# Two-layer transformer with a second mixer block on one core: in the MLP pairs, the high and low half of x go through one 512-column product, and two weight sums move from VectorE to GpSimd

## The chip, the cores and the metric

One core of one Trainium2 chip runs the whole program. The metric is the device time of one launch in microseconds (us); a lower time is better. Engines are called by the profile's names: PE is TensorE (matmul), PEld its weight loads, DVE is VectorE, ACT is ScalarE, POOL is GpSimd, SP the queue that issues most DMAs.

## The reference

The program takes 512 tokens of width 1024 through two layers (an attention mixer and a retention mixer, each followed by an MLP), a final norm, and a further block with a gated feed-forward before and after a sparse-attention and recurrent mixer. The change concerns the squared-ReLU MLP of the first two layers (width 1024, hidden 4096):

```python
def squared_relu_mlp(h, w_up, w_down):
    u = jax.nn.relu(h @ w_up)
    return (u * u) @ w_down
...
h = h + squared_relu_mlp(rms_norm(h, g_mlp[layer]), w_mlp_up[layer], w_mlp_down[layer])
```

All arithmetic is float32. The two gated feed-forward parts (`ffn1`, `ffn2`: silu(h @ w_gate) * (h @ w_up), then w_down, hidden 2816) share some of the code that is touched.

## The kernel before

**Numbers in two parts.** The fast matmul type (fp32r) keeps only part of a float32. So every operand is split: `hi` is the value rounded to fp32r by ScalarE, `lo` is value minus `hi` by VectorE, and a product is w_hi*x_hi + w_hi*x_lo + w_lo*x_hi.

**Pairs and units.** In `mlp0` and `mlp1` the first 8 of the 32 hidden blocks are computed densely. The other 24 blocks are taken in 12 pairs q per layer, by a Strassen-Winograd scheme with seven products, called units, in place of eight: unit p of pair q multiplies a form of the weights (a block, or a sum of blocks, 128 partitions x 512) with a form of x (four 128x256 parts: `x_hi`/`x_lo` for p = 1, 2, 4, the sums `xs_hi`/`xs_lo` for p = 5, 6, 3, 7). One unit in `up_unit` is 12 products of 256 columns: for each of four chunks form_hi * x_hi and form_hi * x_lo (L3134), then four times form_lo * x_hi (L3138). `ffn1` and `ffn2` have 18 such pairs each, made of a gate block and an up block.

**Order.** PE runs the units of a phase in the order of `up_phase`: (q,1), (q-1,4), (q-1,3), (q,2), (q,6), (q,5), (q,7), then (q+1,1), (q,4), (q,3) and so on. An MLP layer has three phases of four pairs. The last two units of a phase stand among the first products of the down projection (`down_part`, L3147, 512 columns); dense down products (L2835, L2840) follow. All waits are hand-written semaphore counts; each engine executes its own list in order.

**Weight forms.** SP loads the blocks of pair q into `forms[q % 2]` (L745 to L754; the last half that the accumulating DMA needs is L751, and it waits until the `lo` of unit (q-2,7) is made). POOL then issues a DMA that adds the second block onto them (`add_forms`, L2791). Two further forms are sums of forms: `third_form` (L1944, for unit 6) and `fourth_form` (L1949, for unit 4), one VectorE instruction of 512 columns each, written to the single buffer `form_sum`. `form_high` (L1039, ACT) writes `ring`, `form_low` (L1937, DVE) writes the `lo`, two units ahead of PE in `up_pairs`.

**Products out of PSUM.** Units 1, 6, 7, 4 of a pair accumulate one after the other in one bank; 2 has its own; 5 and 3 share one. ACT copies the bank after unit 1 (`first_copy`) and after unit 6 (`second_copy`, L1046). DVE makes `first_sum` (L1964, after unit 2), `fourth_sum` (after unit 7: a copy `third_copy` at L1972, then unit 5 minus it, L1974), and `third_sum` (L1980, after unit 3). ACT takes unit 4 straight out of PSUM through ReLU (L1063). Then come ReLU, square and `u_hi` on ACT, `u_lo` on DVE (`up_low`, L1987). PE's unit (q,4) may start only when the copy of (q,7) is made, since it adds onto the same bank; between (q,7) and (q,4) PE has one unit, (q+1,1).

Of the kernel before, what the change touches and what calls it, by code (L numbers as in the profile page):

```python
# [36 lines left out]
P = 128  # L37
# [92 lines left out]
def gates_before(q):  # L130

    return 3 * min(q, PAIR_FROM[2]) + 2 * max(q - PAIR_FROM[2], 0)

# [190 lines left out]
def build(nc, stream, params, tables, tables_ret, tables_mix, x_in, out):  # L324
    with ExitStack() as ctx:
# [15 lines left out]
        x_hi = sb("x_hi", [P, DC, T], F32R)  # L341
        x_lo = sb("x_lo", [P, DC, T], F32R)
# [23 lines left out]
        sq_lo = sb("sq_lo", [P, T], F32R, over=top - T * 4)  # L366
        inv = sb("inv", [P, T])
# [21 lines left out]
        xs_hi = sb("xs_hi", [P, 4, 4, HALF], F32R)  # L389
        xs_lo = sb("xs_lo", [P, 4, 4, HALF], F32R)  # L390
# [12 lines left out]
        third_copy = sb("third_copy", [P, HALF], over=std_final_at)  # L403
# [211 lines left out]
        def x_part(p, j, hi):  # L615
# [3 lines left out]
            return (xs_hi if hi else xs_lo)[:, j, (5, 6, 3, 7).index(p)]  # L619

# [200 lines left out]
        def _(act):  # L821
# [231 lines left out]
            def positive(layer, q, part):  # L1053

                to = up_sum[q % 2]
                made = layer * HIDDEN // P + chunk_of(layer, q, 0)
                if part == 0:
                    act.wait_ge(*upto("f_mm", UNIT_AT[q, 4] + 1))
                    if in_layer(q) >= 2:
                        act.wait_ge(sig("ul_done"), made - 4 + 1)  # L1060
                    else:
                        act.wait_ge(sig("ul_done"), made - 2 * in_layer(q))
                    nc.scalar.activation(to[0][:, HALF:T], ps[:, up_bank(q, 4), 0:HALF], ACT.Relu).then_inc(flag("f_pos"), 1)  # L1063
                elif part == 1:
                    act.wait_ge(*upto("f_ev", 4 * q + 1))
                    nc.scalar.activation(to[0][:, 0:HALF], to[0][:, 0:HALF], ACT.Relu).then_inc(flag("f_pos"), 1)
                else:
                    act.wait_ge(*upto("f_ev", 4 * q + 4))
# [85 lines left out]
            def gate_first(q):  # L1154

                act.wait_ge(*upto("f_ev", 4 * q + 1))
# [513 lines left out]
        def _(dve):  # L1670
# [269 lines left out]
            def third_form(q):  # L1940

                dve.wait_ge(sig(f"added_{q % 2}"), 16 * (q // 2 + 1))
                dve.wait_ge(*upto(f"a_in_{q % 2}", 16 * (q // 2 + 1)))
# [22 lines left out]
            def fourth_sum(layer, q):  # L1966

                if q:
                    dve.wait_ge(*upto("f_ev", 4 * q - 1))
# [1797 lines left out]
```

## Time and profile before

| | |
|---|---|
| median of 3 runs | 2407.51 us (2407.11 to 2408.11) |
| profiled execution | 2407.99 us, its span 2406.2 us |
| PE busy | 2393.8 us, 99% of the span |
| DVE busy | 1627.7 us, 68% |
| ACT busy | 1157.2 us, 48% |
| POOL busy | 155.1 us, 6% |
| granted TensorE clock | 1.00 throughout (the 2.4 GHz level) |
| up units in the MLP layers | 24 pairs x 7 units x 12 products |

A row of a timeline gives the start and the duration in us, the engine, the line, the operation with output <- input, shapes and a count where equal rows are merged, and in brackets the idle time before it with what ended it. The duration of a matmul is its latency: the next one starts long before it ends, so the cost of a product is the distance from start to start. The same holds for DVE instructions, to a smaller degree.

### The profile page before, as it was taken

The page shows a single profiled execution, that of the slowest core. Times are in us where ns is not written, and L with a number is a line of the kernel's source. Part 1 is how long each engine was busy: PE and PEld are TensorE (multiplying, and loading weights), DVE is VectorE, ACT ScalarE, POOL GpSimd, SP SyncE. Part 2 cuts the span into 40 slices and gives each one's busy share as a digit, 9 for nine tenths or more (in the row PEclk, how much of TensorE's full clock was granted, in tenths as well). Part 3 has the DMA queues.
Part 4 walks back from the last instruction along what each step waited for, and adds up shares of the span by engine and source line. Part 5 has one row for each costly group of instructions (what it writes and reads, how often), then busy time and mean ns, then how long its engine had stood idle before and what let it go on. Part 6 is the DMA issues. An engine that isn't in the chain of part 4 may idle for free.

```text
span 2406.2 us, 35737 instructions
## 1 busy us (share of the span) xinstructions
PE 2393.8 (99%) x13500; PEld 2063.6 (86%) x13500; DVE 1627.7 (68%) x2386; ACT 1157.2 (48%) x1837; POOL 155.1 (6%) x151
## 2 busy tenths in 40 slices
PE   9999999999999999999999999999999999999999
PEld 7777898998888888889998889998787778899998
DVE  6777765666656645756666977676968846867664
ACT  3565544554343443535645535454465453544443
POOL 2001000001000000100003000002000001000000
PEclk9999999999999999999999999999999999999999
DMA  4112443533222222444541555552222222455552
GB/s 141 66 66 70 149 149 108 155 106 105 97 79 81 77 79 96 142 133 137 149 132 62 153 153 167 141 158 86 79 71 71 71 70 97 149 158 166 141 154 83
DMA packets 108194, 273.50 MB, mean 114 GB/s; under 512 B 15120, under 2 KB 33808, under 8 KB 107920
## 3 DMA queue, kind: packets, MB, share of 16 engines
q1 hardware_dynamic: 95024, 237.97, 29.2%
q0 software_dynamic: 8640, 31.46, 7.7%
q10 hardware_dynamic: 4384, 2.10, 0.3%
q8 instruction: 94, 1.54, 0.3%
q14 instruction: 52, 0.43, 0.1%
HBM read 269.40 MB, written 2.10 MB: 113 GB/s over the span
## 4 chain that ended last, share of the span: by engine, by line
PE 92%; DVE 4%; issue 2%; ACT 1%; DMA 1%; POOL 1%; SPq 0%; ACTq 0%; DVEq 0%; POOLq 0%
PE ps L2835 29%; PE ps L3134 16%; PE ps L2840 14%; PE ps L3138 8%; PE ps L3147 6%; PE ps L3212 4%; PE ps L3513 2%; PE ps L2904 2%; PE ps L2888 2%; PE ps L3255 1%; PE ps L3039 1%; PE ps L3015 1%; PE ps L2992 1%; PE ps L3242 1%; DMA forms<-in_stream 1%
## 5 line engine op out<-in xcount | busy, mean ns | idle before, releaser
L836 ACT ACTIVATE w_hi<-raw 128x1024 fp32r<-128x1024 f32 x286 | 303.0, 1060 | 765.3 <-PE ps L2840 586.5
L1686 DVE TENSOR_TENSOR w_lo<-raw,w_hi 128x1024 fp32r<-128x1024 f32 x286 | 352.3, 1232 | 112.4 <-ACT w_hi L836 112.0
L2835 PE MATMUL ps<-x_hi,w_hi 128*128 128x512 f32 x848 | 337.2, 398 | 0.3 <-ACT w_hi L836 0.3
L2835 PE MATMUL ps<-x_lo,w_hi 128*128 128x512 f32 x848 | 330.6, 390 | 0.0
L2835 PE MATMUL ps<-u_hi,w_hi 128*128 128x512 f32 x642 | 250.5, 390 | 0.5 <-DVE h L1839 0.5
L2835 PE MATMUL ps<-u_lo,w_hi 128*128 128x512 f32 x642 | 249.9, 389 | 0.0
L3134 PE MATMUL ps<-xs_hi,ring 128*128 128x256 f32 x960 | 240.8, 283 | 1.1 <-ACT second_copy L1046 1.1
L3134 PE MATMUL ps<-xs_lo,ring 128*128 128x256 f32 x960 | 240.7, 283 | 0.0
L1039 ACT ACTIVATE ring<-forms 128x512 fp32r<-128x512 f32 x300 | 187.8, 629 | 92.5 <-PE ps L3138 90.7
L2840 PE MATMUL ps<-x_hi,w_lo 128*128 128x512 f32 x848 | 209.5, 389 | 0.0
L2835 PEld LDWEIGHTS ps<-x_hi,w_hi 128*128 128x128 f32 x848 | 159.3, 188 | 40.4 <-issue 5.8
L2835 PEld LDWEIGHTS ps<-x_lo,w_hi 128*128 128x128 f32 x848 | 159.3, 188 | 33.5 <-issue 1.7
L2840 PEld LDWEIGHTS ps<-x_hi,w_lo 128*128 128x128 f32 x848 | 159.2, 188 | 33.2
L3134 PEld LDWEIGHTS ps<-xs_hi,ring 128*128 128x128 f32 x960 | 184.3, 192 | 1.6 <-issue 1.5
L3134 PEld LDWEIGHTS ps<-xs_lo,ring 128*128 128x128 f32 x960 | 184.3, 192 | 0.1
L3134 PE MATMUL ps<-x_hi,ring 128*128 128x256 f32 x720 | 180.8, 283 | 0.9 <-DVE x_lo L2178 0.6
L3134 PE MATMUL ps<-x_lo,ring 128*128 128x256 f32 x720 | 180.6, 283 | 0.0
L2840 PE MATMUL ps<-u_hi,w_lo 128*128 128x512 f32 x642 | 159.0, 389 | 0.0
L1937 DVE TENSOR_TENSOR ring_b<-forms,ring 128x512 fp32r<-128x512 f32 x224 | 152.5, 684 | 4.2 <-ACT ring L1039 3.9
L2835 PEld LDWEIGHTS ps<-u_hi,w_hi 128*128 128x128 f32 x642 | 120.5, 188 | 26.2 <-DVE h L1839 0.9
L2840 PEld LDWEIGHTS ps<-u_hi,w_lo 128*128 128x128 f32 x642 | 120.5, 188 | 25.0
L2835 PEld LDWEIGHTS ps<-u_lo,w_hi 128*128 128x128 f32 x642 | 120.5, 188 | 24.9
(476 smaller groups left out, 4598.6 us busy)
## 6 DMA issues: line engine op xcount, KB each, us to landing
raw<-in_stream SPq DMA_DIRECT2D x293, 512.0 KB, 3.6
forms<-in_stream SPq DMA_DIRECT2D x180, 256.0 KB, 4.3
forms<-in_stream SPq DMA_DIRECT2D x60, 512.0 KB, 4.7
forms<-in_stream POOLq DMA_DIRECT2D x60, 512.0 KB, 5.7
x_tok<-in_x SPq DMA_DIRECT2D x4, 512.0 KB, 7.2
out_x<-xn ACTq DMA_DIRECT2D x7, 256.0 KB, 2.3
tab_ret<-in_tables_ret SPq DMA_DIRECT2D x1, 1536.0 KB, 6.3
raw<-in_stream SPq DMA_DIRECT2D x3, 256.0 KB, 3.2
```

The lines of the kernel that those rows point to most:

```text
L836: nc.scalar.activation(w_hi[:, slot(n)], raw[:, slot(n)], ACT.Copy).then_inc(hi_done, 1)
L1039: nc.scalar.activation(form_hi[form_slot(v)], form_of(q, p), ACT.Copy).then_inc(flag("f_hi"), 1)
L1686: nc.vector.tensor_tensor(w_lo[:, slot(n)], raw[:, slot(n)], w_hi[:, slot(n)].bitcast(F32), ALU.subtract).then_inc(lo_done, 1)
L1937: nc.vector.tensor_tensor(form_lo[form_slot(v)], form_of(q, p), form_hi[form_slot(v)].bitcast(F32), ALU.subtract).then_inc(flag("f_lo"), 1)
L2835: nc.tensor.matmul(ps[:, gemm_bank(n)], w_hi[:, s, k], x(k), start=(k == 0 and i == 0), stop=False)
L2840: last = nc.tensor.matmul(ps[:, gemm_bank(n)], w_lo[:, s, k], hi(k), start=False, stop=(k == kc - 1))
L2888: return nc.tensor.transpose(dst, src, ident)
L2904: return nc.tensor.matmul(ps[:, VALUE_BANKS[g][tb]], x[:, c, tb * P:(tb + 1) * P], w[:, slot(n), PAIRS * k:PAIRS * (k + 1)].rearrange("p i ...
L3134: nc.tensor.matmul(bank, form_hi[s][:, j * P:(j + 1) * P], x_part(p, j, i == 0), start=(p in (1, 2, 5) and j == 0 and i == 0), stop=False, ...
L3138: last = nc.tensor.matmul(bank, form_lo[s][:, j * P:(j + 1) * P], x_part(p, j, True), start=False, stop=(j == 3), skip_group_check=True)
L3147: last = nc.tensor.matmul(ps[:, gemm_bank(n)], w[:, slot(n), k], x[:, 0, k], start=(k == 0 and i == 0), stop=(k == kc - 1 and i == 2))
L3212: return nc.tensor.matmul(ps[:, RET_BANKS[tb]], x[:, c, tb * P:(tb + 1) * P], weights, start=(c == 0 and w is w_hi and x is x_hi), stop=(c ...
```

## The change

In the MLP layers, five of the seven units (1, 2, 6, 7, 4) become two-sided: x_hi and x_lo, now halves of one tensor, are the moving operand of one 512-column product with form_hi, so that w_hi*x_hi lands in the left half of the PSUM bank and w_hi*x_lo in the right half. The products form_lo * x_hi stay at 256 columns and add onto the left half. The two halves are then added: `first_sum` and `third_sum` become two dependent VectorE instructions each, `fourth_sum`'s copy becomes a `tensor_reduce` over the two halves, and a new `second_sum` does the same for unit 4, whose ReLU on ACT then reads SBUF. ACT's two copies are 512 wide. `third_form` and `fourth_form` move from VectorE's list to GpSimd's, behind the DMA issue of the same pair and ahead of that of the next, in all four layers with pairs. Semaphore counts are adapted. The core of the diff:

```diff
+def sums_before(q):
+    return 7 * min(q, PAIR_FROM[2]) + 4 * max(q - PAIR_FROM[2], 0)
...
-        x_hi = sb("x_hi", [P, DC, T], F32R)
-        x_lo = sb("x_lo", [P, DC, T], F32R)
+        x_two = sb("x_two", [P, 2, DC, T], F32R)
+        x_hi, x_lo = x_two[:, 0], x_two[:, 1]
...
-        xs_hi = sb("xs_hi", [P, 4, 4, HALF], F32R)
-        xs_lo = sb("xs_lo", [P, 4, 4, HALF], F32R)
+        xs_two = sb("xs_two", [P, 2, 4, 4, HALF], F32R)
+        xs_hi, xs_lo = xs_two[:, 0], xs_two[:, 1]
...
-        third_copy = sb("third_copy", [P, HALF], over=std_final_at)
+        first_wide = sb("first_wide", [P, T], over=sq_new_at)
+        second_wide = sb("second_wide", [P, T], over=std_final_at)
+        third_fold = sb("third_fold", [P, HALF], over=inv_at)
...
+        def x_both_parts(p, j):
+            if p in (1, 2, 4):
+                return x_two[:, :, j + (0 if p == 1 else KC // 2), (HALF if p == 4 else 0):(T if p == 4 else HALF)]
+            return xs_two[:, :, j, (5, 6, 3, 7).index(p)]
...
             def copy_of(q, p):
+                if layer_of(q) < 2:
+                    if q:
+                        act.wait_ge(*upto("f_ev", sums_before(q - 1) + (1 if p == 1 else 7)))
+                    nc.scalar.activation((first_wide if p == 1 else second_wide)[:], ps[:, up_bank(q, p)],
+                                         ACT.Copy).then_inc(flag("f_copy"), 1)
...
             def positive(layer, q, part):
                 if part == 0:
-                    act.wait_ge(*upto("f_mm", UNIT_AT[q, 4] + 1))
-                    nc.scalar.activation(to[0][:, HALF:T], ps[:, up_bank(q, 4), 0:HALF], ACT.Relu).then_inc(flag("f_pos"), 1)
+                    act.wait_ge(*upto("f_ev", sums_before(q) + 5))
+                    nc.scalar.activation(to[0][:, HALF:T], to[0][:, HALF:T], ACT.Relu).then_inc(flag("f_pos"), 1)
...
+            def folded(to, wide):
+                nc.vector.tensor_reduce(to, wide.rearrange("p (a f) -> p f a", a=2), AX_X, ALU.add).then_inc(flag("f_ev"), 1)
+            def second_sum(q):
+                whole = wide_of(q, 4)
+                dve.wait_ge(*upto("f_ev", sums_before(q) + 2))
+                folded(up_sum[q % 2][0][:, HALF:T], whole)
...
             def first_sum(layer, q):
-                nc.vector.tensor_tensor(up_sum[q % 2][0][:, 0:HALF], product_of(q, 2), first_copy[:], ALU.add).then_inc(flag("f_ev"), 1)
+                to = up_sum[q % 2][0]
+                nc.vector.tensor_tensor(to, wide_of(q, 2), first_wide[:], ALU.add).then_inc(flag("f_ev"), 1)
+                dve.wait_ge(*upto("f_ev", sums_before(q) + 1))
+                nc.vector.tensor_tensor(to[:, 0:HALF], to[:, 0:HALF], to[:, HALF:T], ALU.add).then_inc(flag("f_ev"), 1)
...
             def fourth_sum(layer, q):
-                nc.vector.tensor_copy(third_copy[:], product_of(q, 7)).then_inc(flag("f_ev"), 1)
-                dve.wait_ge(*upto("f_ev", 4 * q + 2))
-                nc.vector.tensor_tensor(up_sum[q % 2][1][:, HALF:T], product_of(q, 5), third_copy[:], ALU.subtract).then_inc(
+                folded(third_fold[:], wide_of(q, 7))
+                dve.wait_ge(*upto("f_ev", sums_before(q) + 3))
+                nc.vector.tensor_tensor(up_sum[q % 2][1][:, HALF:T], product_of(q, 5), third_fold[:], ALU.subtract).then_inc(
...
             def third_sum(q):
-                nc.vector.tensor_tensor(up_sum[q % 2][1][:, 0:HALF], product_of(q, 3), second_copy[:], ALU.subtract).then_inc(
+                nc.vector.tensor_tensor(to, product_of(q, 3), second_wide[:, 0:HALF], ALU.subtract).then_inc(flag("f_ev"), 1)
+                dve.wait_ge(*upto("f_ev", sums_before(q) + 6))
+                nc.vector.tensor_tensor(to, to, second_wide[:, HALF:T], ALU.subtract).then_inc(flag("f_ev"), 1)
...
                     if before[1] == 2:
                         first_sum(layer, before[0])
+                    if before[1] == 4:
+                        second_sum(before[0])
...
-                    if p == 4 and q + 1 < (layer + 1) * UP_PAIRS:
-                        third_form(q + 1)
...
-                    if p == 3 and q + 1 < (layer + 1) * UP_PAIRS:
-                        fourth_form(q + 1)
...
+            def third_form(q):
+                pool.wait_ge(sig(f"added_{q % 2}"), 16 * (q // 2 + 1))
+                pool.wait_ge(*upto(f"a_in_{q % 2}", 16 * (q // 2 + 1)))
+                if in_layer(q):
+                    pool.wait_ge(*upto("f_lo", UNIT_AT[q - 1, 6] + 1))
+                    pool.wait_ge(*upto("f_sum", 2 * q))
+                nc.gpsimd.tensor_tensor(form_sum[:, 0], forms[q % 2][:, 3], forms[q % 2][:, 0], ALU.add).then_inc(flag("f_sum"), 1)
+            def fourth_form(q):
+                pool.wait_ge(*upto("f_sum", 2 * q + 1))
+                if in_layer(q):
+                    pool.wait_ge(*upto("f_lo", UNIT_AT[q - 1, 4] + 1))
+                nc.gpsimd.tensor_tensor(form_sum[:, 1], forms[q % 2][:, 1], form_sum[:, 0], ALU.add).then_inc(flag("f_sum"), 1)
...
                 for q in range(PAIR_FROM[layer], PAIR_FROM[layer + 1]):
                     add_forms(q)
+                    third_form(q)
+                    fourth_form(q)
...
+                two_sided = wide and p in (1, 2, 6, 7, 4)
...
                 if p == 4:
-                    pe.wait_ge(*upto("f_ev", 4 * q + 2))
+                    pe.wait_ge(*upto("f_ev", sums_before(q) + (3 if wide else 2)))
...
                 for j in range(4):
+                    if two_sided:
+                        nc.tensor.matmul(both, form_hi[s][:, j * P:(j + 1) * P], x_both_parts(p, j),
+                                         start=(p in (1, 2) and j == 0), stop=False, skip_group_check=True)
-                    for i in range(2):
+                    for i in range(0 if two_sided else 2):
                         nc.tensor.matmul(bank, form_hi[s][:, j * P:(j + 1) * P], x_part(p, j, i == 0),
                                          start=(p in (1, 2, 5) and j == 0 and i == 0), stop=False, skip_group_check=True)
```

## Rows read from the trace of the kernel before

**Rows 1.** The page's part 1: busy us, share of the span, instructions.
```profile
PE 2393.8 (99%) x13500; PEld 2063.6 (86%) x13500; DVE 1627.7 (68%) x2386; ACT 1157.2 (48%) x1837; POOL 155.1 (6%) x151
```

**Rows 2.** Waits of PE by line, whole run: us, times, longest; largest in pairs.
```profile
PE ps L3134 <- ACT second_copy L1046: 1.1, 2, 0.6
```

**Rows 3.** Windows, first MLP phase: us, busy us of each engine, clock, DMA.
```profile
332.50:372.70 40.20, 40.20 (x325) 39.71 (x325) 32.16 (x57) 29.94 (x58) 3.45 (x4) 1.00 0.67 187
```

**Rows 4.** Timeline of PE: starts of units, of dense blocks, and between both.
```profile
359.91 0.28 PE L3134 MATMUL ps<-x_hi,ring 128*128 128x256 f32 x1
...
361.35 0.28 PE L3134 MATMUL ps<-x_hi,ring 128*128 128x256 f32 x1
...
369.99 1.09 PE L3147 MATMUL ps<-u_hi,w_hi 128*128 128x512 f32 x4
...
374.17 0.28 PE L3134 MATMUL ps<-xs_hi,ring 128*128 128x256 f32 x1
...
383.80 0.39 PE L2835 MATMUL ps<-u_hi,w_hi 128*128 128x512 f32 x1
...
389.24 0.39 PE L2835 MATMUL ps<-u_hi,w_hi 128*128 128x512 f32 x1
...
606.90 1.98 PE L3212 MATMUL ps<-w_hi,x_hi 128*128 128x512 f32 x8
608.72 1.98 PE L3212 MATMUL ps<-w_hi,x_lo 128*128 128x512 f32 x8
```

**Rows 5.** Timeline of DVE, around the end of unit (2,7) at 359.91.
```profile
358.16 0.69 DVE L1937 TENSOR_TENSOR ring<-form_sum,ring 128x512 fp32r<-128x512 f32 x1 [0.65 <-ACT ring L1039]
358.77 0.69 DVE L1987 TENSOR_TENSOR u_lo<-inv_final,u_hi 128x512 fp32r<-128x512 f32 x1
360.21 0.43 DVE L1972 COPY third_copy<-ps 128x256 f32<-128x256 f32 x1 [0.75 <-PE ps L3138]
360.67 0.43 DVE L1974 TENSOR_TENSOR inv_final<-ps,third_copy 128x256 f32<-128x256 f32 x1
361.01 0.68 DVE L1937 TENSOR_TENSOR ring_b<-forms,ring 128x512 fp32r<-128x512 f32 x1
361.61 0.68 DVE L1944 TENSOR_TENSOR form_sum<-forms 128x512 f32<-128x512 f32 x1
```

**Rows 6.** Timelines of POOL and DVE where additions of both meet.
```profile
236.65 0.74 DVE L1713 SCALAR_TENSOR_TENSOR x_lo<-h,prm,x_hi 128x512 fp32r<-128x512 f32 x1
...
236.69 1.85 POOL L2786 TENSOR_TENSOR rstd<-rstd,xn 128x512 f32<-128x512 f32 x1 [3.57 <-ACT xn L857]
...
237.31 1.51 DVE L1869 TENSOR_TENSOR x_sum<-x_fp 128x256 f32<-128x256 f32 x1
...
1293.46 1.29 POOL L2786 TENSOR_TENSOR sq_new<-sq_new,xn 128x512 f32<-128x512 f32 x1
...
1293.68 0.69 DVE L1885 TENSOR_TENSOR down<-ps,inv_sq 128x512 f32<-128x512 f32 x1 [1.33 <-PE ps L2840]
...
1294.47 0.83 DVE L1887 TENSOR_TENSOR h<-h,down 128x512 f32<-128x512 f32 x1
```

**Rows 7.** Load of pair 3 (SP), its adding DMA (POOL), and L2791's landing times.
```profile
346.86 0.33 SPq L751 DMA_DIRECT2D forms<-in_stream  x1
...
352.21 0.86 POOL L2791 DMA_DIRECT2D forms<-in_stream  x1 [8.04 <-DMA forms<-in_stream]
...
DMA to landing us min/median/max: 5.1/5.7/8.8
```

**Rows 8.** Same, pair 4: load issue on SP and adding DMA on POOL.
```profile
356.94 0.33 SPq L751 DMA_DIRECT2D forms<-in_stream  x1
...
360.88 0.86 POOL L2791 DMA_DIRECT2D forms<-in_stream  x1 [7.80 <-DMA forms<-in_stream]
```

**Rows 9.** Timeline at the phase's end: last u_lo, and the product that needs it.
```profile
378.33 0.69 DVE L1987 TENSOR_TENSOR u_lo<-u,u_hi 128x512 fp32r<-128x512 f32 x1 [1.43 <-ACT u_hi L1082]
...
380.39 0.39 PE L3147 MATMUL ps<-u_hi,w_hi 128*128 128x512 f32 x1
```

**Rows 10.** Timeline of DVE in ffn1: the copy after unit 7 there.
```profile
1501.42 0.42 DVE L2077 COPY last_copy<-ps 128x256 f32<-128x256 f32 x1 [0.75 <-PE ps L3138]
```

More of the change, by code:

```diff
@@ L366, in build @@
         sq_lo = sb("sq_lo", [P, T], F32R, over=top - T * 4)
+        inv_at = where[0]
         inv = sb("inv", [P, T])
@@ L1154, in gate_first @@
             def gate_first(q):
-                act.wait_ge(*upto("f_ev", 4 * q + 1))
+                act.wait_ge(*upto("f_ev", sums_before(q) + 1))
                 part = gate_up[q % 2][0][:, 0:HALF]
@@ L1938, in form_low @@
                                         ALU.subtract).then_inc(flag("f_lo"), 1)
-            def third_form(q):
-                dve.wait_ge(sig(f"added_{q % 2}"), 16 * (q // 2 + 1))
-                dve.wait_ge(*upto(f"a_in_{q % 2}", 16 * (q // 2 + 1)))
-                nc.vector.tensor_tensor(form_sum[:, 0], forms[q % 2][:, 3], forms[q % 2][:, 0], ALU.add).then_inc(flag("f_sum"), 1)
-            def fourth_form(q):
-                dve.wait_ge(*upto("f_sum", 2 * q + 1))
-                nc.vector.tensor_tensor(form_sum[:, 1], forms[q % 2][:, 1], form_sum[:, 0], ALU.add).then_inc(flag("f_sum"), 1)
             def product_of(q, p):
@@ L2021, in up_pairs @@
                 if more:
-                    third_form(q + 1)
                     form_low(v + 3)
+                second_sum(q)
                 third_sum(q)
@@ L2026, in up_pairs @@
                 up_low(layer, q, 1)
-                if more:
-                    fourth_form(q + 1)
             def mlp(first, chunks_before, norm, next_norm):
@@ L2047, in mlp @@
                         x_forms(norm, c + 2)
-                third_form(layer * UP_PAIRS)
-                fourth_form(layer * UP_PAIRS)
                 form_low(UNIT_FROM[layer])
@@ L2115, in gate_pairs @@
                         up_first_sum(before[0])
-                    if p == 4 and q + 1 < PAIR_FROM[layer + 1]:
-                        third_form(q + 1)
                     if v + 2 < end and v + 2 > UNIT_FROM[layer] + 3:
                         form_low(v + 2)
-                    if p == 3 and q + 1 < PAIR_FROM[layer + 1]:
-                        fourth_form(q + 1)
                     if p == 6 and q > qs[0]:
@@ L2138, in gate_pairs @@
                     form_low(v + 2)
-                    third_form(q + 1)
                     form_low(v + 3)
@@ L2143, in gate_pairs @@
                 hidden_low(layer, q)
-                if more:
-                    fourth_form(q + 1)
             def x_normed(layer, norm, j, parts):
@@ L2214, in ffn @@
                         x_gate_forms_low(layer, 3)
-                        third_form(PAIR_FROM[layer])
                         for i in range(3):
@@ L2220, in ffn @@
                         form_low(v + 3)
-                        fourth_form(PAIR_FROM[layer])
                     dve.wait_ge(sig("ul_done"), CHUNKS_FROM[layer] + c)
@@ L3107, in up_unit @@
                 q, p = UNITS[v]
-                bank = ps[:, up_bank(q, p), 0:HALF]
+                bank, both = ps[:, up_bank(q, p), 0:HALF], ps[:, up_bank(q, p)].rearrange("p (a f) -> p a f", a=2)
                 layer = layer_of(q)
+                wide = layer < 2
+                two_sided = wide and p in (1, 2, 6, 7, 4)
                 two_back = q - 2 if in_layer(q) >= 2 else None
```

40 lines of the change are left out of this document (19 added, 21 removed).

## The prediction

> **What bounds the kernel now.** I read the engine shares first [rows 1]: PE is busy 99% of the span, DVE 68%. Durations of matmuls overlap, so "busy" alone doesn't prove that PE never waits; the list of PE's waits does. Its largest entry in the pair units is 1.1 us in two places [rows 2]. In the first MLP phase (units of pairs 0 to 3) PE is busy 40.20 of 40.20 us and DVE 32.16, which is 80% [rows 3]. So these phases are bound by how fast PE starts products, and DVE is the next engine, with 20% to spare.
>
> The price of a product is the distance between starts, not the 0.28 or 0.39 us that a row prints. A unit starts at 359.91 and the next at 361.35: 1.44 us for 12 products of 256 columns, 120.0 ns each. A dense block starts at 383.80 and the next at 389.24: 5.44 us for 24 products of 512 columns, 226.7 ns each [rows 4]. The difference, 106.7 ns, is 256 columns at 2.4 GHz, the level at which the clock stands [rows 3]. What is left is 13.3 ns per product, whatever its width. Someone who takes 2 x 0.28 - 0.39 = 0.17 us from the durations would expect 480 x 0.17 = 82 us from this change; those durations contain the pipeline's latency, which is paid once per stream.
>
> **1. Merged products.** Removed: in 24 pairs, 5 units each, 8 products of 256 become 4 of 512. 4 x (2 x 120.0 - 226.7) = 53 ns per unit, and 120 units make 6.4 us. That is the upper end. Against it stands the change of width inside a unit. Between 369.99 and 374.17 PE runs 12 products of 512 and 12 of 256, entered from 256: 4.18 us, where 12 x 226.7 + 12 x 120.0 = 4.16 [rows 4]. So a change to 512 and back costs about 20 ns, and each merged unit has one. 53 - 20 = 33 ns, x 120 = 4.0 us, the value I take, because it is the only row with such a change. The moving operand now comes in two pieces of 256. The nearest row is L3212, whose moving operand is cut into four pieces: 8 products in 1.82 us, 227.5 ns each [rows 4], so pieces cost nothing visible. New lengths: a merged unit 1.407 us, a pair 5 x 1.407 + 2 x 1.44 = 9.92 us in place of 10.08.
>
> The Trainium skill, in "TensorE: Matmul & The Clock Gate", section "Back-to-back issue gap", gives 131 ns as the sustained spacing at 512 columns and 81 ns at 128; a straight line between them puts 256 near 98 ns, and merging would save 65 ns x 480 = 31 us, called an estimate from that page. The same section's other formula, N/2.4 + 2.5 ns, would make it 2.5 ns x 480 = 1.2 us. The trace agrees with neither: it shows 226.7 and 120.0, and the sum goes by those.
>
> **2. DVE's list in an MLP pair.** Start-to-start prices [rows 5]: an addition of 512 columns 0.60 us (361.01 to 361.61), of 256 columns 0.34 (360.67 to 361.01), and 0.12 more where the next one needs its result (360.21 to 360.67 is 0.46). A 512-column step that reads PSUM has the same duration, 0.69, as one that doesn't [rows 6], so I give it 0.60 too. Before: 7 `form_low`, 2 `up_low`, 2 form sums, 11 x 0.60 = 6.60; the copy 0.46; three sums 1.02; together 8.08 of 10.08, which is the 80% of rows 3. After: 9 x 0.60 = 5.40; `first_sum` 0.60 + 0.12 + 0.34 = 1.06; `fourth_sum` 0.72 + 0.34 = 1.06; `second_sum` 0.60; `third_sum` 0.46 + 0.34 = 0.80. Together 8.92 of 9.92. That fits, with 1.0 us left.
>
> No row shows a `tensor_reduce`. Its floor is what the copy of half the width costs (0.34), since it reads twice as much; its ceiling I set at double the 512-column addition, 1.20. I take 0.60, the row for the same number of elements read. The Trainium skill, in "VectorE: DVE Perf Modes", section on the perf-mode tier table, lists `tensor_reduce` as running at the plain rate only; no run here shows it.
>
> **3. The two form sums on POOL.** Alone, a POOL addition of 512 columns takes 1.28 to 1.29 us (1293.46). What matters is what it does to DVE. POOL starts one at 236.69 while DVE runs L1713, and takes 1.85: it waited about 0.57. The next DVE addition, at 237.31, takes 1.51 us where a 256-column one takes 0.43 [rows 5, 6]: it stood still about 1.09 us. L1887 at 1294.47 takes 0.83 in place of 0.69 and gets going 1.15 us after POOL's start. But L1885 at 1293.68, which reads PSUM and one SBUF operand, takes its normal 0.69 in the midst of POOL's addition [rows 6]. So: a POOL addition shuts out DVE steps with two SBUF inputs for about 1.14 us; the one that starts first goes first; steps out of PSUM pass. The Trainium skill states this rule in "SBUF — State Buffer", section "Who interferes with whom", and adds that `tensor_reduce` never contends on this chip; the first part agrees with rows 6, the second no run here shows.
>
> DVE thus gives up 2 x 0.60 and may get back 2 x 1.14 = 2.28 us of standing still per pair. If all of it falls on steps with two SBUF inputs, DVE needs 8.92 + 2.28 = 11.20 us in a pair of 9.92, and DVE is the bound. If it falls on DVE's idle time and on its steps out of PSUM (together about 1.0 + 2.8 us of a pair), it is free.
>
> **When POOL runs them.** `third_form` of pair q starts when the added block has landed: L751 to the POOL issue is 5.35 us for pair 3 and 3.94 for pair 4, and the landing takes 5.7 more [rows 7, 8]. L751 goes out when the `lo` of (q-2,7) is ready, so the landing is about 0 to 2 us before unit (q,1) starts. That is where DVE has its idle time (0.65 before 358.16, 0.75 before 360.21 [rows 5]) but also two `lo` steps, and behind them the step with the tightest due time. This step is the sum over (q,7)'s halves. PE has one unit, now 1.407 us, to run before (q,4). DVE wakes 0.30 us after the end of (q,7) (359.91 to 360.21 [rows 4, 5]), and the reduce takes 0.69 and some 0.05 for the signal: 1.04. It may start at most 0.37 us late before PE waits.
>
> I walked DVE's, POOL's and PE's lists through a phase with these prices. Pairs 0 and 1: no wait; `fourth_form(1)` meets the PSUM steps. Pair 2, with its landing early or late, puts DVE behind, and `fourth_form(3)`, which waits for the `lo` of (2,4), can only start just as DVE reaches (2,7)'s sum. The `up_low` ahead of that sum is held, and PE waits 0.04, 0.22 or 1.31 us at (2,4), by whether pair 3's block lands before or after DVE passes (3,1). At (3,4) four chunks of the down projection, 12 x 0.227 = 2.7 us, cover the delay. I take 0.7 us per phase, the middle; 6 phases make +4.2 us.
>
> **4. Other edits.** ACT: two copies 256 wider, about +0.25 us each, in a list that is busy 29.94 of 40.20 [rows 3]; covered. Unit 4's ReLU now stands behind DVE's `second_sum`, and behind it on ACT are `form_high` of (q,5) and (q,7); in my walk they are ready 0.4 us ahead of need. If DVE falls back more than that, PE waits here too. POOL's next DMA issue stands behind `fourth_form`; it moves by at most 1 us, which only shifts the landing. End of a phase: `third_sum` is 0.46 longer and the last u_lo ends at 379.02, needed at 380.39 [rows 9]: 1.37 in hand, 0. `ffn1`/`ffn2`: 36 pairs lose 1.2 us of DVE work and gain the 2.28; the copy after unit 7 waits 0.75 us on PE there and takes only 0.42 [rows 10], and PE's unit is still 1.44, so 0.
>
> **Sum.** 2407.99 - 4.0 + 4.2 = 2408.2 for the profiled execution, which stands 0.5 above the median: 2407.7 us.
>
> **Rivals.**
> A, the forecast: gain and waits cancel, 2403 to 2412. Chance 0.47.
> B, POOL's additions find the gaps: no late sum. For it: both idle stretches of DVE lie where the block lands [rows 5]. Then -4.0 to -6.4: 2401.1 to 2403.5. Chance 0.23; the part beyond -4.8 us is 0.13.
> C, DVE becomes the bound (slower). Place: the sum over (q,7)'s halves, behind held `lo` steps. It decides once more than 1.0 us of the 2.28 falls on steps with two SBUF inputs. The stretches between the first three sums of a phase are uncovered: 2 x (11.20 - 9.92) - 0.37 = 2.2 us per phase, 13 in all, less 4.0: 2416.7. Against it: 2.8 us per pair are PSUM steps that pass. Chance 0.18.
> D, the reduce costs 1.20: then 0.30 + 1.29 + 0.05 = 1.64 us stand against 1.407 even when DVE is idle, and DVE's list grows by 1.2: 18 uncovered sums at about 1 us each, less 4.0: about 2421. Chance 0.08.
> E, the 512-column product with two halves is no cheaper than two: gain 0, waits 4.2: 2411.7. Against it L3212. Chance 0.04, counted as no change.
>
> **Range and chances.** A measurement of this kernel can tell about 0.2%, 4.8 us, from no change. Faster by more: 0.13, from B. Slower: C and D, 0.26. Within: 0.61. 2402 leaves out the best part of B (under 0.1), 2419 leaves out D and the far end of C (about 0.1).
>
> **What would show it.** Right: merged products 227 ns apart, unit starts 1.39 to 1.41 apart, PE's waits on the sum over (q,7) 1 us or less at the third pair of a phase. DVE rows with two SBUF inputs of up to 1.8 us beside POOL's additions. Wrong: unit starts 1.44 apart (E); PE waits at every pair (C); a reduce of over 0.8 us (D); no waits (B). A wait of PE on `form_high` would be a miss of part 4.

## The result, and the profile of the changed kernel

The changed kernel takes 2420.18 us (median of 4 runs, 2417.2 to 2422.2); beside it the kernel before took 2407.69 (2407.1 to 2408.1). The ratio is 1.0052, with a 95% interval of 1.004 to 1.0063: slower by 0.5%, and 1.2 us above the upper end of the range that I gave (2402 to 2419). The profiled execution has a span of 2420.0 us, against 2406.2 before: 13.8 us more. The changed kernel also spreads over 5 us from run to run, where the one before spreads over 1. Of the eleven executions of four_early_dve below, two took 3381 and 8462 us; they are left out of its median.

The page's part 1, which answers to [rows 1]: PE has 480 products fewer, DVE is busy 39 us longer although 120 form sums have left it for 72 new steps, and POOL has doubled.

```profile
PE 2394.9 (99%) x13020; PEld 2039.2 (84%) x13020; DVE 1666.6 (69%) x2338; ACT 1160.6 (48%) x1837; POOL 329.3 (14%) x271
```

The list of PE's waits, which answers to [rows 2] (us in total, times, longest). All of these waits are new. L3162 is the merged product, L3178 the down projection's `down_part`, L3165 an unmerged product, L2861 a dense block.

```profile
PE ps L3162 <- ACT second_wide L1061: 4.1, 5, 1.2
PE ps L3178 <- DVE u_lo L2010: 4.0, 4, 1.8
...
PE ps L3162 <- DVE third_fold L1966: 1.9, 4, 0.6
PE ps L2861 <- DVE u_act L1712: 1.3, 1, 1.3
...
PE ps L3165 <- DVE last_copy L2094: 1.1, 2, 0.6
```

The window of [rows 3], the first MLP phase. PE had been busy for all of its 40.20 us, DVE for 32.16 and POOL for 3.45.

```profile
332.50:372.70 40.20, 38.45 (x242) 34.19 (x241) 37.95 (x59) 29.90 (x56) 12.93 (x11) 1.00 0.68 182
```

PE around unit (2,7), which answers to [rows 4]. A row of L3162 holds a unit's four merged products, one of L3169 its low group. The unit begun at 360.54 is followed by the next at 361.94, 1.40 us later: merging works as priced. But (2,7), at 359.08, waited 1.17 us.

```profile
357.27 0.64 PE L3169 MATMUL ps<-xs_two,ring_b 128*128 128x256 f32 x4
359.08 1.16 PE L3162 MATMUL ps<-xs_two,ring 128*128 128x512 f32 x4 [1.17 <-ACT second_wide L1061]
360.07 0.64 PE L3169 MATMUL ps<-xs_two,ring_b 128*128 128x256 f32 x4
360.54 1.09 PE L3162 MATMUL ps<-x_two,ring 128*128 128x512 f32 x4
361.47 0.63 PE L3169 MATMUL ps<-x_two,ring_b 128*128 128x256 f32 x4
361.94 1.09 PE L3162 MATMUL ps<-x_two,ring 128*128 128x512 f32 x4
```

What made it wait, read backwards over three engines. ACT made `second_wide` at 358.36, the eighth of a chain of steps without a gap that began at 355.12. There ACT had stood 1.71 us, since its list has unit 4's relu next, and that one needs DVE's `second_sum`:

```profile
352.26 0.64 ACT L1053 ACTIVATE ring<-form_sum 128x512 fp32r<-128x512 f32 x1 [0.92 <-POOL form_sum L2809]
...
355.12 0.42 ACT L1077 ACTIVATE u<-u 128x256 f32<-128x256 f32 x1 [1.71 <-DVE u L1966]
355.44 0.62 ACT L1053 ACTIVATE ring<-forms 128x512 fp32r<-128x512 f32 x1
...
358.36 0.57 ACT L1061 ACTIVATE second_wide<-ps 128x512 f32<-128x512 f32 x1
```

DVE (first three rows) took from 350.40 to 354.41 for two `form_low` (printed as one row of x2) and one `up_low`: 4.0 us for 3 x 0.60. POOL (last two) ran both form sums in that time.

```profile
350.40 2.38 DVE L1951 TENSOR_TENSOR ring_b<-forms,ring 128x512 fp32r<-128x512 f32 x2
352.70 1.78 DVE L2010 TENSOR_TENSOR u_lo<-u_act,u_hi 128x512 fp32r<-128x512 f32 x1
354.41 0.68 DVE L1966 TENSOR_REDUCE u<-ps 128x256 f32<-128x512 f32 x1
...
350.80 1.42 POOL L2809 TENSOR_TENSOR form_sum<-forms 128x512 f32<-128x512 f32 x1 [6.91 <-DMA forms<-in_stream]
352.30 1.63 POOL L2816 TENSOR_TENSOR form_sum<-forms,form_sum 128x512 f32<-128x512 f32 x1
```

The excess is 2.2 us for two additions, 1.1 each: the price of [rows 6]. Nothing of these two additions fell into a gap. ACT also waited 0.92 us, until 352.26, for the first form sum itself, but after that it still stood 1.71 us for DVE's `second_sum`: the late form sum is not what set the time here.

The second place is the end of a phase. In phase 2 of the second layer PE wants its first `down_part` at 1195.77, after the low group of (19,7) begun at 1195.29. It gets `u_lo` at 1197.7, since POOL's `fourth_form` (1195.45) holds the `up_low` that makes it. The DVE step two places ahead (1193.51) had already taken 1.79 us beside POOL's `third_form`, which began at 1193.47; so both additions of the pair stand in this wait:

```profile
1193.51 1.79 DVE L1951 TENSOR_TENSOR ring_b<-form_sum,ring 128x512 fp32r<-128x512 f32 x1
...
1195.83 1.75 DVE L2010 TENSOR_TENSOR u_lo<-u,u_hi 128x512 fp32r<-128x512 f32 x1
...
1195.45 1.58 POOL L2816 TENSOR_TENSOR form_sum<-forms,form_sum 128x512 f32<-128x512 f32 x1 [0.69 <-DVE ring_b L1951]
...
1197.73 1.15 PE L3178 MATMUL ps<-u_hi,w_hi 128*128 128x512 f32 x4 [1.80 <-DVE u_lo L2010]
1198.72 1.68 PE L3178 MATMUL ps<-u_lo,w_hi 128*128 128x512 f32 x4
1200.19 1.91 PE L3178 MATMUL ps<-u_hi,w_lo 128*128 128x512 f32 x4
1201.90 1.32 PE L3162 MATMUL ps<-x_two,ring 128*128 128x512 f32 x4
```

After this wait the products themselves are slow, and the window shows why: the last but two column, the mean granted clock, is 0.58 there: for most of the stretch it stood at 1.2 GHz and not at 2.4.

```profile
1199.00:1203.00 4.00, 4.00 (x12) 3.15 (x11) 2.17 (x4) 0.00 (x0) 0.00 (x0) 0.58 0.77 131
```

### The profile page after: what moved, and what is told of

Same layout as the page of the kernel before. It is cut to its first block, busy times and chain, and to the rows that moved or that the text cites. A ratio compares the mean times of both kernels' runs of the same rounds, so it can differ in the third digit from the quotient of the medians.

```text
span 2420.0 us, 34960 instructions
## 1 busy us (share of the span) xinstructions
PE 2394.9 (99%) x13020; PEld 2039.2 (84%) x13020; DVE 1666.6 (69%) x2338; ACT 1160.6 (48%) x1837; POOL 329.3 (14%) x271
## 4 chain that ended last, share of the span: by engine, by line
PE 89%; DVE 6%; issue 2%; ACT 2%; POOL 1%; DMA 0%; ACTq 0%; DVEq 0%; SPq 0%; POOLq 0%
PE ps L2861 29%; PE ps L2866 14%; PE ps L3165 11%; PE ps L3169 7%; PE ps L3178 6%; PE ps L3243 4%; PE ps L3162 3%; PE ps L3544 2%; PE ps L2930 2%; PE ps L2914 2%; PE ps L3286 1%; PE ps L3065 1%; DVE ring_b L1951 1%; PE ps L3041 1%; PE ps L3018 1%
## 5 line engine op out<-in xcount | busy, mean ns | idle before, releaser
L2861 PE MATMUL ps<-x_two,w_hi 128*128 128x512 f32 x1696 | 410.0, 394 | 2.1 <-DVE u_act L1712 1.3
L2861 PEld LDWEIGHTS ps<-x_two,w_hi 128*128 128x128 f32 x1696 | 315.0, 188 | 76.0 <-issue 9.1
L2861 PE MATMUL ps<-u_hi,w_hi 128*128 128x512 f32 x642 | 250.5, 390 | 0.3 <-DVE h L1853 0.3
L2861 PE MATMUL ps<-u_lo,w_hi 128*128 128x512 f32 x642 | 249.9, 389 | 0.0
L3165 PE MATMUL ps<-xs_two,ring 128*128 128x256 f32 x1536 | 215.6, 283 | 1.1 <-ACT second_copy L1065 1.1
L2866 PE MATMUL ps<-x_two,w_lo 128*128 128x512 f32 x848 | 209.5, 389 | 0.0
L3165 PEld LDWEIGHTS ps<-xs_two,ring 128*128 128x128 f32 x1536 | 198.0, 192 | 1.6 <-issue 1.5
L2809 POOL TENSOR_TENSOR form_sum<-forms 128x512 f32<-128x512 f32 x60 | 87.8, 1463 | 803.7 <-DVE ring_b L1951 514.1
L2866 PEld LDWEIGHTS ps<-x_two,w_lo 128*128 128x128 f32 x848 | 159.2, 188 | 33.1
L2861 PEld LDWEIGHTS ps<-u_hi,w_hi 128*128 128x128 f32 x642 | 120.5, 188 | 25.9 <-DVE h L1853 0.7
L2861 PEld LDWEIGHTS ps<-u_lo,w_hi 128*128 128x128 f32 x642 | 120.5, 188 | 24.9
L3165 PE MATMUL ps<-x_two,ring 128*128 128x256 f32 x864 | 121.7, 284 | 2.0 <-DVE last_copy L2094 1.1
L3169 PE MATMUL ps<-xs_two,ring_b 128*128 128x256 f32 x760 | 121.9, 283 | 0.0
L3165 PEld LDWEIGHTS ps<-x_two,ring 128*128 128x128 f32 x864 | 112.0, 192 | 3.9 <-issue 3.1
```

The costliest lines, as they stand in the source:

```text
L2809: nc.gpsimd.tensor_tensor(form_sum[:, 0], forms[q % 2][:, 3], forms[q % 2][:, 0], ALU.add).then_inc(flag("f_sum"), 1)
L2861: nc.tensor.matmul(ps[:, gemm_bank(n)], w_hi[:, s, k], x(k), start=(k == 0 and i == 0), stop=False)
L2866: last = nc.tensor.matmul(ps[:, gemm_bank(n)], w_lo[:, s, k], hi(k), start=False, stop=(k == kc - 1))
L3165: nc.tensor.matmul(bank, form_hi[s][:, j * P:(j + 1) * P], x_part(p, j, i == 0), start=(p in (1, 2, 5) and j == 0 and i == 0), stop=False, ...
L3169: last = nc.tensor.matmul(bank, form_lo[s][:, j * P:(j + 1) * P], x_part(p, j, True), start=False, stop=(j == 3), skip_group_check=True)
```

## The experiments

Below, H is the theory that POOL's additions hold DVE's steps with two SBUF inputs, and L that DVE's own new list is too long. Line numbers of a fence are those of that kernel. Beside these runs the kernel before stood at 2407.1 to 2407.5 us.

**pool_write_only.** Is it the addition on POOL, or only that POOL does something?

```diff
-nc.gpsimd.tensor_tensor(form_sum[:, 0], forms[q % 2][:, 3], forms[q % 2][:, 0], ALU.add).then_inc(flag("f_sum"), 1)
+nc.gpsimd.memset(form_sum[:, 0], 0.5).then_inc(flag("f_sum"), 1)
```

(the same for `form_sum[:, 1]`)

> The changed kernel with GpSimd's two additions per pair replaced by fills of the same 512 columns, which read nothing from SBUF. Waits and order stay as they are; the two form sums are left out (units 6 and 4 use a constant). Theory H: steps of VectorE keep their 0.6 us beside them, no waits of PE in the pairs, 2403 to 2405 us. Theory L: 2412 or more, as VectorE's list is unchanged.

Measured: 2402.25 us (2401.7 to 2403.0), ratio 0.9978 [0.9969, 0.9988], span 2401.2. As H said. None of PE's waits above is left. The page's part 1, then DVE in the stretch shown above, with both writes of POOL in it:

```profile
PE 2389.1 (99%) x13020; PEld 2037.3 (85%) x13020; DVE 1605.3 (67%) x2338; ACT 1163.1 (48%) x1837; POOL 217.4 (9%) x271
```

```profile
350.38 1.28 DVE L1951 TENSOR_TENSOR ring_b<-forms,ring 128x512 fp32r<-128x512 f32 x2
351.58 0.68 DVE L2010 TENSOR_TENSOR u_lo<-u_act,u_hi 128x512 fp32r<-128x512 f32 x1
352.18 0.68 DVE L1966 TENSOR_REDUCE u<-ps 128x256 f32<-128x512 f32 x1
...
350.83 0.53 POOL L2809 MEMSET form_sum<- 128x512 f32 x1 [6.69 <-DMA forms<-in_stream]
351.41 0.53 POOL L2816 MEMSET form_sum<- 128x512 f32 x1
```

The same three steps take 1.80 us instead of 4.01, and no single `form_low` or `up_low` of this trace prints more than 0.69 us. DVE is busy 1605.3 us in all, 61.3 less than with additions, or 0.51 us for each of the 120: almost half of the 1.14 that one can cost. This run also splits the change in two. Set against the kernel before, the difference of unit starts goes from -0.35 us at the first unit, (0,1), to -4.98 at (24,5), the first unit behind the MLP layers: 4.6 us for 120 merged units, 0.039 each. Set against the changed kernel the span is 18.8 us shorter; 0.6 us of that lies in a stretch of `ffn1` that varies between traces anyway (see the table below), the rest where the additions stand. A write is shorter than an addition too (0.53 against 1.28 us), so this run alone can't tell a held DVE from a form sum that is merely made earlier. The rows above can: the steps that PE waited for are DVE's own, 1.1 us too long each. A GpSimd instruction of 1.28 us that reads no SBUF was not run.

**pool_copy_only.** Does a POOL instruction with one input hold DVE too?

```diff
-nc.gpsimd.tensor_tensor(form_sum[:, 0], forms[q % 2][:, 3], forms[q % 2][:, 0], ALU.add).then_inc(flag("f_sum"), 1)
+nc.gpsimd.tensor_copy(form_sum[:, 0], forms[q % 2][:, 3]).then_inc(flag("f_sum"), 1)
```

(and `forms[q % 2][:, 1]` into `form_sum[:, 1]`)

> The changed kernel with GpSimd's two additions a pair replaced by copies of one input of 512 columns (the sums are left out, the forms themselves are passed on). With plain writes in their place the time was 2402.25 us and VectorE was not held. Theory R (a GpSimd instruction that reads SBUF holds VectorE's two-input steps, however many inputs it has): VectorE's steps show 1.3 us and more again and the time is above 2408 us. Theory R2 (only GpSimd's two-input instructions do): 2402 to 2403 us.

Measured: 2404.57 us (2403.6 to 2405.9), span 2402.5. Neither theory's number: a copy does hold DVE, as R says, but it takes only 0.61 us and so costs little, 2.3 us more than plain writes. The page, and the same place once more, DVE then POOL:

```profile
PE 2389.1 (99%) x13020; PEld 2037.3 (85%) x13020; DVE 1621.0 (67%) x2338; ACT 1162.0 (48%) x1837; POOL 248.2 (10%) x271
```

```profile
350.29 1.64 DVE L1951 TENSOR_TENSOR ring_b<-forms,ring 128x512 fp32r<-128x512 f32 x2
...
350.17 0.61 POOL L2816 COPY form_sum<-forms 128x512 f32<-128x512 f32 x1
```

DVE's pair takes 1.64 us instead of 1.28, and its busy time rises by 15.7 us, 0.13 for each copy. R2, "only two-input instructions hold", is refuted; R was right on the hold and wrong on the time.

**merged_dve_forms.** The merged products without POOL: both form sums back in DVE's list at their old places.

```diff
+                    if p == 4 and q + 1 < (layer + 1) * UP_PAIRS:
+                        third_form(q + 1)
                     if v + 2 < end:
                         form_low(v + 2)
+                    if p == 3 and q + 1 < (layer + 1) * UP_PAIRS:
+                        fourth_form(q + 1)
...
```

(and likewise at a phase's end and in `ffn1` and `ffn2`; GpSimd's two calls are gone)

> The changed kernel with the two form sums back on VectorE, as in the kernel before; the 512-column products and the longer sums stay. Theory H (GpSimd's additions hold VectorE's steps with two SBUF inputs): nothing is held any more, so PE's waits in the MLP phases go and the 4 us of the merged products remain: 2403 to 2406 us. Theory L (VectorE's own list has become too long): its list is 8.92 + 2 x 0.60 = 10.12 us against a pair of 9.92, longer than in the changed kernel without holding, so it stays at 2412 or more.

Measured: 2409.8 us (2409.0 to 2411.8), ratio 1.0011 [1.0001, 1.002], span 2407.4: between both theories. There is one new kind of wait, six times, once at the first `down_part` of each phase; its list row, then DVE and PE at the first of them:

```profile
PE ps L3205 <- DVE u_lo L2021: 3.5, 6, 0.6
```

```profile
369.10 0.68 DVE L2021 TENSOR_TENSOR u_lo<-u,u_hi 128x512 fp32r<-128x512 f32 x1
...
369.93 1.16 PE L3205 MATMUL ps<-u_hi,w_hi 128*128 128x512 f32 x4 [0.59 <-DVE u_lo L2021]
```

DVE's list is 8.92 + 1.20 = 10.12 us against a pair of 9.92. The lag grows by 0.2 us a pair, and the phase's first down chunks meet it. So L has a share too, which the changed kernel hides, as POOL has taken the 1.20 us away. DVE is busy 1673.6 us in this run: the 120 form sums are worth 68.3 us of it (1605.3 with writes on POOL), and on POOL their hold put 61.3 back, so the move relieved DVE by 7 us in all.

**pool_forms_only.** The other half alone: the kernel before, with `third_form` and `fourth_form` called from POOL's `add_layer`.

> The kernel before with only the two form sums moved to GpSimd; products and sums as before. Theory H: VectorE needs 6.88 + 2.28 = 9.16 us of 10.08, so most pairs don't wait, but u_lo and the lo of forms next to a phase's end and the dense blocks at the start of ffn2 are still held: 2410 to 2414 us. Theory L: VectorE's list is shorter than ever, nothing waits: 2407.5 or a little less.

Measured: 2410.98 us (2410.4 to 2412.9), ratio 1.0015 [1.0006, 1.0025], span 2408.6. As H said, and at one of the two places that it named, the start of `ffn2`; at the phases' ends the list shows no wait. In the MLP pairs DVE's list of 8.08 less 1.20, 6.88 us, leaves room for the 2.28. The loss is in the gated layers: `last_copy` (1.1 us in two waits) and the dense start of `ffn2` (1.3 and 0.8).

**pool_mlp_only.** The changed kernel with the form sums of `ffn1` and `ffn2` on DVE again.

```diff
-                    third_form(q)
-                    fourth_form(q)
+                    if layer < 2:
+                        third_form(q)
+                        fourth_form(q)
...
```

(the rest puts the calls back into VectorE's lists of `ffn1` and `ffn2`)

> The changed kernel with the form sums on GpSimd only in the two MLP layers and on VectorE in ffn1 and ffn2. In the trace of the changed kernel PE is 10.5 us behind the kernel before when ffn1's pairs begin and 13.8 us at the end. Theory H: the 3.3 us of ffn1 and ffn2 go, 2416 to 2418 us. Theory L (all of it in the MLP layers' sums, the rest chance): no change from 2420.

Measured: 2418.57 us (2414.6 to 2419.2), ratio 1.0046 [1.0029, 1.0063], span 2412.8. The gated layers' waits are gone. The medians of this kernel and the change differ by 1.6 us only and their runs overlap, so this time doesn't decide between the two theories, and the waits' price is read from the traces.

**early_low_dve.** merged_dve_forms with one step earlier:

```diff
-                    if p == 7 and q > qs[0] + 1:
+                    if p == 5 and q > qs[0] + 1:
                         up_low(layer, q - 2, 1)
```

> The merged products with the form sums on VectorE (2409.8 us), and the step up_low(q - 2, 1) moved in VectorE's list from the turn of unit (q, 7) to that of (q, 5). Nothing is left out. Theory P (place): the six waits of 0.53 to 0.60 us at the first chunks of the down projection stand there only because this step comes after form_low and fourth_sum in the list, though its input was ready four units earlier; they go, and the time is 2409.8 - 3.5 = 2406.3 us, faster than before by about 1 us. Theory L (load): VectorE's list of 10.12 us a pair is longer than the pair of 9.92 us, so the lateness comes up at another step instead: 2408.5 to 2410 us, and new waits on folded or form_lo in the last pair of each phase.

Measured: 2405.45 us (2404.8 to 2407.0), ratio 0.9994 [0.9984, 1.0003], span 2403.5. The six waits are gone, for 4.4 us, and P holds. The lag is not: each phase gains 0.3 to 0.4 us on the kernel before, where the run with plain writes gains 0.75 to 0.80, and it loses 0.10 to 0.27 us at a time at its last unit 7 and unit 4.

**early_low_pool, act_later_pool, both_moves_pool.** The same move in the changed kernel; ScalarE's side moved instead, as below; and both.

```diff
-                    if before and before[1] == 4:
-                        positive(layer, before[0], 0)
+                    if q > qs[0] and p == 5:
+                        positive(layer, q - 1, 0)
+                        squared(q - 1, 0)
                     if v + 3 < end:
                         form_high(v + 3)
...
-                    if q > qs[0] and p == 6:
-                        squared(q - 1, 0)
```

> The changed kernel, form sums on GpSimd, with up_low(q - 2, 1) moved from the turn of unit (q, 7) to that of (q, 5) in VectorE's list. Nothing is left out. Theory P: the waits of the first down chunks on u_lo (4.0 us in all) and the low clock behind the longest of them (about 1.6 us) go, and the time is 2420.2 - 5.6 = 2414.6 us. Theory S (shared debt): VectorE, held by GpSimd's additions, is late whichever step is asked for first; the wait that goes there comes back at the fold or at the copy of unit 6 some microseconds later, and the time stays at 2417 us or more.

> The changed kernel with ScalarE's positive(q - 1, 0) moved in its list from the turn of unit (q - 1, 3) to that of (q, 5), behind the copy of unit (q, 6), and squared(q - 1, 0) right behind it. Nothing is left out. Theory P: unit (q, 7) no longer waits for VectorE's second_sum through ScalarE's list; the four or five waits of 1.2 us (4.1 us in all) go, and the time is 2420.2 - 4.1 = 2416.1 us. Theory S: VectorE's lateness is then met by the fold at (q, 4) or by u_lo, which is made later too as its high half is later, and the time stays at 2418 us or more.

> The changed kernel with both moves: up_low(q - 2, 1) earlier in VectorE's list and positive(q - 1, 0) later in ScalarE's. Nothing is left out. Theory P: places add up, 2420.2 - 4.1 - 5.6 = 2410.5 us, with fold waits of about 2 us and those of the two gated layers left. Theory S: less than the sum of the two single moves, 2415 us or more.

Measured: 2415.6 us (2413.4 to 2416.2), 2420.65 (2418.3 to 2422.5) and 2414.73 (2412.6 to 2416.8). Their waits of PE in the lists, in this order:

```profile
PE ps L3162 <- ACT second_wide L1061: 5.7, 8, 1.2
...
PE ps L3178 <- DVE u_lo L2010: 0.5, 1, 0.5
```

```profile
PE ps L3177 <- DVE u_lo L2009: 6.0, 6, 1.8
PE ps L3161 <- DVE third_fold L1965: 4.8, 6, 1.6
```

```profile
PE ps L3161 <- DVE third_fold L1965: 2.9, 6, 1.5
...
PE ps L3177 <- DVE u_lo L2009: 1.9, 5, 0.6
```

The earlier `up_low` gives 4.6 us, nearer to the 5.6 of theory P than to S, although the waits on `second_wide` grow from 4.1 to 5.7. Taking away ACT's way gives nothing: its 4.1 us come back at the fold and at `u_lo`, as theory S said. Both together give 5.5 us, not 9.7. So the way through ACT was where PE first met DVE's lateness, and not a cost beside it. What is left, 7 us and more above the kernel before, is the lateness itself.

**four_merged_dve, four_merged_pool.** Less work for DVE: unit 4 keeps its eight products of 256 columns, ACT's relu reads it from PSUM as before, `second_sum` is gone, and the counts of DVE's sums go from 7 to 6 a pair. The line that chooses the units:

```diff
...
-                two_sided = wide and p in (1, 2, 6, 7, 4)
+                two_sided = wide and p in (1, 2, 6, 7)
...
```

> Form sums on VectorE, up_low where the change has it, but only four of the seven units merged (1, 2, 6, 7): unit 4 keeps its two products of 256 columns and ScalarE's relu takes it from PSUM as before, so VectorE's second_sum of 0.60 us a pair is not there. Nothing is left out. Theory L (VectorE's own list sets the end of a phase): its list is 9.52 us against a pair of about 9.96, no lag builds up, and the time is that of before less 24 x 4 x 0.035 = 3.4 us, 2404 us, with no loss at units (3, 7) and (3, 4). Theory P (only the place of up_low): the place is the old one here, so the waits of 0.5 to 0.6 us at the first down chunks are there again, and the time is 2406.5 to 2408 us.

> The same four merged units with the form sums on GpSimd as the change has them. Nothing is left out. Theory L: what VectorE lacks is time, 8.32 us of its own and 2 x 1.14 us held, 10.6 us a pair against 11.2 with five units; half of the lag of 1.24 us a pair is gone and the time falls to 2411 to 2415 us. Theory S (the hold falls where it hurts, whatever the sum): the fold and u_lo wait as before and only the way through ScalarE is gone, 2417 to 2419 us.

Measured: with the sums on DVE 2405.05 us (2404.3 to 2405.9), ratio 0.9989 [0.998, 0.9998]; with them on POOL 2414.94 (2409.6 to 2417.0), ratio 1.003 [1.0019, 1.004]. Both are nearer to L. The first is 4.8 us better than five merged units with the same places, though it merges less; no wait is listed in the MLP phases, and the units gain 0.15 us a pair. But L's "no loss" is not quite so: at the last unit 4 of each phase 0.15 to 0.19 us is lost, as the first down chunks still come 0.1 us late. The second is 5.2 us better than the change, at the upper end of the range that L gave; waits of 2.7 us on `u_lo` and 1.5 on the fold remain.

**four_early_dve.** Both remedies: four merged units, the form sums on DVE, `up_low` at `p == 5`.

> Four merged units (1, 2, 6, 7), form sums on VectorE, and up_low(q - 2, 1) moved from the turn of unit (q, 7) to that of (q, 5). Nothing is left out. With four units merged alone, the first down chunks of a phase still started 0.10 us late (369.48 after a group of 256 columns begun at 368.90, where 0.48 is the step), right at the end of that u_lo. Theory P (the place is a cost of its own, beside the load): the six starts gain 0.1 us each and what follows them another 0.07, and the time is 2404 to 2404.7 us. Theory L (with the list short enough the place is worth nothing): no change from 2405.05 us.

Measured: 2403.27 us (2403.05 to 2404.08), ratio 0.9984 [0.9974, 0.9994], span 2402.3. P holds, and the time is below even its range: 1.8 us below four_merged_dve, of which its starts and what follows them give 0.17 us a phase, 1.0 in all; the rest was not traced. This is the best version that computes everything: 0.16% faster than before, and 0.7% faster than the change. Set against the kernel before, unit starts move from +0.26 us at the first unit to -3.27 at (24,5), 3.5 us for 96 merged units, and each phase gains 0.59, so none of it is lost at a phase's end.

## Why the prediction was wrong, point by point

The span grew by 13.8 us; the sum had +0.2. Where the additions' 18.8 us fall, read as the difference of unit starts between the changed kernel and the one that only writes:

| stretch | loss, us | my term |
|---|---|---|
| MLP layer 1, phases 1, 2, 3 | 2.6, 1.1, 2.2 | 0.7 each |
| MLP layer 2, phases 1, 2, 3 | 2.9, 4.5, 2.2 | 0.7 each |
| `ffn1` | 1.4 | 0 |
| `ffn2` | 2.0 | 0 |

Of the 1.4 in `ffn1`, 0.6 lie between units (27,3) and (28,1). That stretch takes 42.3 to 43.1 us in the traces of all these kernels, with the sums on either engine, as one wait of up to 0.5 us for DVE's `h` comes and goes; this part is not the additions'.

**Merged products (part 1): right.** 0.039 us per unit against 0.033, 4.6 us against 4.0; units start 1.40 to 1.41 us apart. Rival E falls.

**DVE's list (part 2): right.** The reduce of 512 columns out of PSUM takes 0.68 to 0.69 us and the next step starts 0.60 to 0.73 after it, as I took it. Rival D falls.

**The price of one addition (part 3): right.** 1.1 us for each of two in a row, measured above. And it is the cause: with plain writes in its place the loss is gone.

**The walk through a phase: mis-sized, and this is the largest error.** 4.2 us stood for what measured 15.4. By unit starts, 5.4 of the 15.4 us stand at unit 7 and the unit ahead of it, 6.6 at the first down chunks with the low clock behind them, 2.6 at unit 4 behind the fold. The step fails in two places. First, I walked the list with the landing as before and took the middle of 0.04, 0.22 and 1.31 us for one wait at (2,4). In the trace both form sums for the next pair fell on DVE steps with two SBUF inputs while pair 1 ended, and the loss was 1.4 us at once: at (2,7), and in the same way at (10,7) and (22,7), each the unit 7 of a phase's third pair. The high end of my walk, 1.31 us, is close to that by luck: it stood for a wait at (2,4) through the fold, and this one, at (2,7) through ACT, is another. Three of the six phases have it. Second, "at (3,4) four chunks of the down projection cover the delay" is wrong. Those chunks don't cover DVE, they wait for it: `down_part` begins with a wait for `up_low(q - 2, 1)`, which stands in DVE's list just ahead of the sum. That wait was 0.22, 0.22, 1.78 and 1.80 us in the first two phases of each layer. I had looked at who waits for the sum and not at who waits for the step before it. merged_dve_forms shows the same wait without POOL.

**ACT's list (part 4): wrong in place, of little weight in time.** I had `form_high` 0.4 us ahead of need and wrote that PE would wait here if DVE fell back more. It did, through the relu that now follows `second_sum`, but on the copy of unit 6 rather than on `form_high`: 4.1 us of listed waits. act_later_pool shows that this is not 4.1 us to be won.

**`ffn1` and `ffn2` at 0: wrong, 3.4 us against the kernel before.** 1.6 of it stand at the copy after unit 7, 2.0 at the start of `ffn2`, and the stretch of `ffn1` that varies gave 0.2 back. The 0.75 us that the copy after unit 7 had in hand [rows 10] covers one addition only in part: two waits of 0.6 us. And I had not looked at the dense start of `ffn2`, where no pair runs but the first form sums do. DVE then POOL then PE there:

```profile
2081.44 1.78 DVE L2162 SCALAR_TENSOR_TENSOR x_even<-h,prm,inv 128x512 f32<-128x512 f32 x1
2083.15 1.78 DVE L2200 TENSOR_TENSOR u_lo<-u,u_hi 128x512 fp32r<-128x512 f32 x1
...
2080.14 2.53 POOL L2809 TENSOR_TENSOR form_sum<-forms 128x512 f32<-128x512 f32 x1 [4.49 <-DMA forms<-in_stream]
...
2085.68 2.55 PE L2861 MATMUL ps<-x_two,w_hi 128*128 128x512 f32 x10 [1.26 <-DVE u_act L1712]
```

Two steps that take 0.74 and 0.69 us elsewhere take 1.78 each, and PE waits 1.26 us for what follows them.

**The clock: not in the sum, 1.6 us (counted in the 15.4).** From 1198.72 to 1203.05 PE starts 12 products of 512 columns in 4.33 us, where the same 12 after the wait at 1111.65 take 2.75.

**The rivals.** C had the right size (2416.7, at 0.18): it priced every addition in full between the first sums of a phase. Its place, the sum over (q,7)'s halves, was the smallest of three. B, that POOL finds the gaps, is what pool_forms_only shows in the MLP layers of the kernel before; in the changed kernel DVE's list beside them is 8.92 us a pair, not 6.88, and it no longer holds.

**What stays open.** The changed kernel's spread of 5 us: when a block lands decides what an addition meets, and a wait near 1.8 us can be followed by a low clock or not; how much each adds to the spread was not measured.

## What to carry to other kernels

An engine that is 80% busy has room for its own work, not for being held: count a GpSimd instruction that reads SBUF on VectorE's list too, here 1.1 us for one of 1.28 where the VectorE steps around it have two SBUF inputs, and 0.51 on average. Before calling a delay covered, list what the covering work itself waits for, the steps just ahead of the late one included. And a change need not be taken whole: with the form sums kept on VectorE, the unit left unmerged that cost VectorE 0.60 us for a gain of 0.039, and one step asked for earlier, a change that lost 12.5 us became one that gains 3.8.

## What the runs showed of the hardware

The hold goes by whether GpSimd reads SBUF. For 120 instructions of 512 columns VectorE's busy time rises, counted from the run with writes (whose 512-column steps print 0.69 us at most), by 0.13 us each with one-input copies of 0.61 us and by 0.51 us each with additions of 1.28. The Trainium skill, "SBUF — State Buffer", section "Who interferes with whom", says the same: a VectorE step with two SBUF inputs contends with a GpSimd instruction that reads SBUF, and not with one that only writes it.

Steps out of PSUM pass, the reduce too. POOL's addition began at 360.84. DVE's steps at 360.81 and 361.54 read PSUM and keep their 0.69 and 0.42 us; only the third, the `form_low` pair at 361.88, is long, with POOL's next addition, from 362.20, beside it:

```profile
360.81 0.69 DVE L1966 TENSOR_REDUCE third_fold<-ps 128x256 f32<-128x512 f32 x1
361.54 0.42 DVE L1995 TENSOR_TENSOR inv_final<-ps,third_fold 128x256 f32<-128x256 f32 x1
361.88 2.49 DVE L1951 TENSOR_TENSOR ring_b<-forms,ring 128x512 fp32r<-128x512 f32 x2
...
360.84 1.28 POOL L2809 TENSOR_TENSOR form_sum<-forms 128x512 f32<-128x512 f32 x1 [6.09 <-DMA forms<-in_stream]
```

The same section says that `tensor_reduce` never contends on this chip; this row agrees for a reduce that reads PSUM, and no `tensor_reduce` in this trace reads SBUF.

The clock can fall after a short wait and need not: in the changed kernel PE stood 1.78 us at 1111.65 and 1.80 us at 1197.73, both at the same place of a phase. The first was followed by products 0.23 us apart, the second by a stretch with a mean granted clock of 0.58 between 1199 and 1203, the clock having stood at 1.00 before both. In act_later_pool a wait of 1.83 us at 1112.55 was followed by the low clock too: 12 products in 4.32 us, and a mean granted clock of 0.60 between 1114 and 1118. The two waits of 1.60 us in that trace were not.
